# Mixture-of-experts output: rows weighted as they leave PSUM and added by an accumulating scatter to a copy of the residual in device memory

## What is computed

```
weights = g_val * e_val / sum(e_val)         # two experts of 32 for each token
y = 0
for e in range(32):
    h = silu(x2d @ w_gate[e]) * (x2d @ w_up[e])        # 1024 -> 256
    y = y + combine[:, e:e + 1] * (h @ w_down[e])      # 256 -> 1024
h = h + y                                    # the residual rows
return rmsnorm(h, final_norm_g)              # then the second block
```

## Time and profile before

| | |
|---|---|
| median of 3 runs | 1476.79 us (1476.45 to 1480.57) |
| the profiled execution | 1477.63 us, span 1475.9 us |
| PE | busy 1288.1 us, 87% of the span |
| DVE, ACT, POOL | 564.3, 479.1 and 173.1 us |
| TensorE clock granted | 0.933 of full speed in the mean |
| expert loop | from 537.95 us (first turned rows) to 790.58 us (last output stored) |

### The profile page before, as it was taken

How to read it: one execution, slowest core, us unless ns; L and a number is a source line. 1 busy time by engine, 2 the same in 40 slices (tenths; PEclk the granted TensorE clock), 3 DMA queues, 4 the chain that set the end, 5 groups by cost and what they waited for, 6 DMA issues and landing times. The chain is left out here.

```text
span 1475.9 us, 24366 instructions
## 1 busy us (share of the span) xinstructions
PE 1288.1 (87%) x10299; PEld 998.4 (68%) x10299; DVE 564.3 (38%) x1010; ACT 479.1 (32%) x806; POOL 173.1 (12%) x219
## 2 busy tenths in 40 slices
PE   5999797579986949998883699999989989899988
PEld 4888753269966735654442698888877767666668
DVE  3331132765653132322223513344438753522222
ACT  4222266612134221111112424555545533111120
POOL 4000032010004012322211001122200000000030
PEclk9999899789997969998987799999999999999989
DMA  4332000000017559999996346233152026113011
GB/s 144 114 100 72 1 0 0 14 3 4 4 59 287 201 193 367 386 390 394 390 405 228 90 152 135 77 100 96 58 73 71 30 91 226 57 57 114 0 58 58
DMA packets 92488, 195.53 MB, mean 132 GB/s; under 512 B 9510, under 2 KB 73084, under 8 KB 79452
## 3 DMA queue, kind: packets, MB, share of 16 engines
q1 hardware_dynamic: 86604, 183.48, 36.5%
q0 software_dynamic: 5200, 8.40, 1.8%
q10 hardware_dynamic: 576, 2.10, 0.4%
HBM read 184.74 MB, written 16.81 MB: 137 GB/s over the span
## 5 line engine op out<-in xcount | busy, mean ns | idle before, releaser
L1768 PE MATMUL hidden_ps<-w_gate,gathered_t 128*64 128x256 f32 x432 | 116.4, 430 | 24.1 <-DMA w_up<-exp_w_up_dram 23.3
L1768 PE MATMUL hidden_ps<-w_up,gathered_t 128*64 128x256 f32 x432 | 116.4, 430 | 0.0
L1768 PEld LDWEIGHTS hidden_ps<-w_gate,gathered_t 128*64 128x64 f32 x432 | 64.8, 156 | 62.6 <-issue 36.8
L1333 PE MATMUL wo_ps<-w_out_high,wo_x_high 128*128 128x256 f32 x256 | 75.2, 294 | 19.2 <-POOL wo_x_low L1374 19.2
L414 PE MATMUL proj_ps<-block_in_high,w_in_low 128*128 128x512 f32 x232 | 90.5, 390 | 0.0
L414 PE MATMUL proj_ps<-block_in_low,w_in_high 128*128 128x512 f32 x232 | 90.5, 390 | 0.0
L414 PE MATMUL proj_ps<-block_in_high,w_in_high 128*128 128x512 f32 x232 | 90.4, 390 | 0.0
L462 DVE TENSOR_TENSOR w_in_low<-w_in_raw,w_in_high 128x2048 fp32r<-128x2048 f32 x20 | 45.8, 2292 | 116.4 <-ACT w_in_high L454 116.4
L414 PE MATMUL gate_ps<-block_in_high,gate_w_high 128*128 128x512 f32 x192 | 79.8, 416 | 11.3 <-DVE gate_w_low L462 11.3
L414 PE MATMUL gate_ps<-block_in_low,gate_w_high 128*128 128x512 f32 x192 | 76.5, 398 | 0.0
L414 PE MATMUL gate_ps<-block_in_high,gate_w_low 128*128 128x512 f32 x192 | 76.3, 397 | 0.0
(11 more groups left out here) (456 smaller groups left out, 3147.2 us busy)
## 6 DMA issues: line engine op xcount, KB each, us to landing
w_gate<-exp_w_gate_dram SPq DMA_DIRECT2D x27, 1024.0 KB
w_up<-exp_w_up_dram SPq DMA_DIRECT2D x27, 1024.0 KB
w_down<-exp_w_down_dram SPq DMA_DIRECT2D x27, 1024.0 KB
w_in_raw<-w_in_dram SPq DMA_DIRECT2D x20, 1024.0 KB, 5.7
slot_scratch_and_keys<-w_in_dram SPq DMA_DIRECT2D x14, 1024.0 KB, 5.3
vb<-w_in_dram SPq DMA_DIRECT2D x6, 1024.0 KB, 5.6
gate_w_raw_odd<-w_in_dram SPq DMA_DIRECT2D x6, 1024.0 KB, 5.9
slot_scratch_and_keys<-exp_w_gate_dram SPq DMA_DIRECT2D x5, 1024.0 KB
```

Source lines behind the costliest of these rows:

```text
L1333: m = pe.matmul(banks[n % nb][:, 0:UNIT], x[a][k][:, c * P:(c + 1) * P], wts.parts(u, k, slice(0, UNIT))[b], start=(k == 0 and a + b == 0) ...
L1768: x = pe.matmul(g_bank[e % 2][a * CAP:(a + 1) * CAP, 0:DE], xT[e % 2][:, k, :], w[:, k, :], start=(k == 0), stop=(k == KC - 1))
```

## The change

Rows leave PSUM already multiplied with the weight of their token and expert, and the scatter adds them to rows of `token_sums_dram`, a tensor of 512 rows which starts as a copy of `h`. In its parts:

- SP writes `h` (2 MB) to `token_sums_dram` behind the last weight load of the out projection; POOL waits for it at the head of `experts`.
- The lists keep only the token's row. The second value of the marks is 1, is multiplied with the choice's weight (DVE), and a second product on PE (`weigh`, 16 matmuls, as two copies for the two halves of the partitions) gives the weight for each place: `list_weights`. It is made before the loop and again at the end of a round.
- DVE's copy becomes a multiply by a column, and ACT's copy gets a scale.
- POOL's scatter adds (`compute_op=ALU.add`). Two experts can add to the same row, so each scatter waits for the one before it.
- SP reads back 4 x 512 KB straight into `h`. The eight additions on DVE are gone; ACT squares as the chunks land.

```diff
@@ out_projection, SP; Router
                     head.store_rows(sp)
                     load_expert(sp, A, M, 5, 5)
+                    head.store_sums(sp)
+    def store_sums(self, sp):
+        sp.dma_start(self.M["sums_dram"].rearrange("(c p) d -> p c d", p=P), self.h[:, :, :]).then_inc(self.M["sums_in"], 16)
@@ Lists
     def product(self, pe, n, at, bank):
-            x = pe.matmul(bank[0:CAP, 0:2 * NE], at[:, jc, :], self.M["marks"][:, jc, :, :].rearrange("p a e -> p (a e)"),
-                          start=(jc == 0), stop=(jc == 2 * TT - 1))
+            x = pe.matmul(bank[0:CAP, 0:NE], at[:, jc, :], self.M["marks"][:, jc, 0, :], start=(jc == 0), stop=(jc == 2 * TT - 1))
+    def weigh(self, pe, n, at, bank):
+        pe.wait_ge(self.marked, n + 1)
+        for a in range(2):
+            for jc in range(2 * TT):
+                x = pe.matmul(bank[a * CAP:(a + 1) * CAP, NE:2 * NE], at[:, jc, :], self.M["marks"][:, jc, 1, :],
+                              start=(jc == 0), stop=(jc == 2 * TT - 1))
+        x.then_inc(self.weighed, 1)
+    def mark_first(self, dve, at):
+        pl = self.M["places"][:, :, :].rearrange("p j c -> p (j c)")
+        dve.tensor_scalar(pl, pl, float(CAP), None, ALU.add).then_inc(self.back, 1)
+        dve.wait_ge(self.back, 1)
+        self.mark(dve, 1, at)
+    def store_weights(self, dve, n, bank):
+        dve.wait_ge(self.weighed, n + 1)
+        dve.tensor_copy(self.weights[:, :], bank[:, NE:2 * NE]).then_inc(self.weights_in, 1)
@@ experts, SP
-                    sp.dma_start(yg[c], rows[:, c, :, :]).then_inc(got[c], 16)
+                    sp.dma_start(h[:, c, :], rows[:, c, :]).then_inc(got[c], 16)
@@ experts, POOL
+                def add_rows(e):
+                    return pool.indirect_dma_start(out=M["sums_dram"], out_offset=bass.IndirectOffsetOnAxis(ap=idx[:, e:e + 1], axis=0),
+                                                   in_=y[e % YB][:, :], in_offset=None, bounds_check=S - 1, oob_is_err=False,
+                                                   compute_op=ALU.add).then_inc(y_out[e % YB], 16)
+                pool.wait_ge(M["sums_in"], 16)
...
-                            write_rows(idx[:, e, 1:2], e)
+                            if e:
+                                pool.wait_ge(y_out[(e - 1) % YB], uses(rnd, e - 1, YB) * 16 + 16)
+                                pool.sem_inc(seen)
+                            add_rows(e)
@@ experts, PE
+                pe.wait_ge(marked, 1)
+                lists.weigh(pe, 1, at[:, :, :], h_bank[0])
                 with pe.Fori(0, rounds(pe)) as rnd:
...
-                    lists.product(pe, rnd + 1, at[:, :, :], h_bank[0])
+                    lists.weigh(pe, rnd + 2, at[:, :, :], h_bank[0])
+                    lists.product(pe, rnd + 2, at[:, :, :], h_bank[0])
@@ experts, ACT
-                    act.activation(y[e % YB][:, 512:D], y_bank[e % 2][CAP:P, :], ACT.Copy).then_inc(y_hi, 1)
+                    act.activation(y[e % YB][:, 512:D], y_bank[e % 2][CAP:P, :], ACT.Copy,
+                                   scale=lists.weights[CAP:P, e:e + 1]).then_inc(y_hi, 1)
@@ experts, DVE
-                    dve.tensor_copy(y[e % YB][:, 0:512], y_bank[e % 2][0:CAP, :]).then_inc(y_lo, 1)
+                    dve.tensor_scalar(y[e % YB][:, 0:512], y_bank[e % 2][0:CAP, :], lists.weights[0:CAP, e:e + 1], None, ALU.mult).then_inc(y_lo, 1)
...
+                    hot = M["marks"][:, :, 1, :]
+                    dve.tensor_tensor(hot, hot, w[:, :, :].rearrange("p j c -> p (j c)").unsqueeze(2).to_broadcast([P, 2 * TT, NE]),
+                                      ALU.mult).then_inc(marked, 1)
...
-                        dve.scalar_tensor_tensor(out=h[:, c, :], in0=yg[c][:, j, :], scalar=M["weights"][:, j, c:c + 1], in1=h[:, c, :],
-                                                 op0=ALU.mult, op1=ALU.add).then_inc(added, 1)
```

More of the change, by code:

```diff
@@ L1586, in __init__ @@
         self.M = M
-        self.idx = s.sb_right("list_places", [CAP, NE, 2], I32)
-        self.offs, self.placed = s.sb_right("place_offsets", [CAP, 2, NE]), s.sb_right("placed", [CAP, 2, NE])
+        self.idx = s.sb_right("list_places", [CAP, NE], I32)
+        self.offs, self.placed = s.sb_right("place_offsets", [CAP, NE]), s.sb_right("placed", [CAP, NE])
+        self.weights = s.sb_right("list_weights", [P, NE])
         self.xg = [s.sb_right(f"gathered{j}", [CAP, D]) for j in range(GB)]
@@ L1591, in __init__ @@
             s.sem("places_" + n) for n in ("marked", "less", "listed", "shifted", "stored"))
+        self.weighed, self.weights_in, self.back = s.sem("list_weights_ready"), s.sem("list_weights_stored"), s.sem("places_put_back")
         self.zeroed, self.offs_made, self.x_in = s.sem("gathered_zeroed"), s.sem("offsets_made"), s.sems("tokens_gathered", GB)
@@ L1674, in experts @@
         fin_g = M["up"][5][:, :, :].rearrange("p k n -> p (k n)")[:, 0:D]
-        rows = y_dram[0:2 * S, :].rearrange("(c p k) d -> p c k d", p=P, k=2)
-        yg = [M["gate"][j][:, :, :].rearrange("p k n -> p (k n)").rearrange("p (a d) -> p a d", a=2) for j in (4, 5, 0, 2)]
+        rows = M["sums_dram"].rearrange("(c p) d -> p c d", p=P)
         sq = [M["up"][j][:, :, :].rearrange("p k n -> p (k n)")[:, 0:D] for j in (4, 0)]
@@ L1715, in _ @@
                 for c in range(TT):
-                    sp.dma_start(yg[c], rows[:, c, :, :]).then_inc(got[c], 16)
+                    sp.dma_start(h[:, c, :], rows[:, c, :]).then_inc(got[c], 16)
             @block.gpsimd
             def _(pool):
-                def write_rows(places, e):
-                    return pool.indirect_dma_start(out=y_dram, out_offset=bass.IndirectOffsetOnAxis(ap=places, axis=0),
-                                                   in_=y[e % YB][:, :], in_offset=None, bounds_check=2 * S - 1,
-                                                   oob_is_err=False).then_inc(y_out[e % YB], 16)
+                def add_rows(e):
[3 more added lines that the diff above has]
+                pool.wait_ge(M["sums_in"], 16)
                 pool.sem_inc(places_free)
@@ L1878, in choice_weights @@
                     dve.wait_ge(weighed, 6)
+                    hot = M["marks"][:, :, 1, :]
+                    dve.tensor_tensor(hot, hot, w[:, :, :].rearrange("p j c -> p (j c)").unsqueeze(2).to_broadcast([P, 2 * TT, NE]),
+                                      ALU.mult).then_inc(marked, 1)
                 choice_weights()
+                lists.mark_first(dve, at[:, :, :])
+                lists.store_weights(dve, 0, h_bank[0])
+                dve.wait_ge(lists.weights_in, 1)
                 dve.wait_ge(M["gain_in"], 16)
@@ L1896, in _ @@
                     dve.wait_ge(places_free, rnd + 2)
-                    lists.mark(dve, rnd + 1, at[:, :, :])
+                    lists.mark(dve, rnd + 2, at[:, :, :])
                     lists.store(dve, rnd + 1, h_bank[0])
+                    lists.store_weights(dve, rnd + 1, h_bank[0])
                 dve.wait_ge(gain_in, 16)
@@ L1904, in gain @@
                     dve.tensor_tensor(h[:, c, :], h[:, c, :], fin_g, ALU.mult).then_inc(gained, 1)
-                for c in range(TT):
-                    dve.wait_ge(got[c], 16)
-                    for j in range(2):
-                        if j:
-                            dve.wait_ge(added, 2 * c + 1)
-                        dve.scalar_tensor_tensor(out=h[:, c, :], in0=yg[c][:, j, :], scalar=M["weights"][:, j, c:c + 1], in1=h[:, c, :],
-                                                 op0=ALU.mult, op1=ALU.add).then_inc(added, 1)
-                    if c:
-                        gain(c - 1)
+                for c in range(1, TT):
+                    gain(c - 1)
                 dve.wait_ge(squared, TT)
```

24 lines of the change are left out of this document (12 added, 12 removed).

## The result

| | before | changed |
|---|---|---|
| median of 4 runs each | 1477.0 us (1476.45 to 1480.57) | 1499.49 us (1493.25 to 1501.55) |
| ratio | 1 | 1.0147, 95% interval 1.0123 to 1.0172 |
| the profiled execution | 1477.63 us, span 1475.9 | 1500.56 us, span 1499.1 |
| TensorE clock granted, mean | 0.933 | 0.929 |

The change costs 22.5 us, 1.5%, and the interval is clear of 1. The forecast had the direction and a range that holds the time (1474 to 1515), but a sum of +10.6, less than half of what came.

What follows compares the result with a forecast made beforehand. The prediction took the DMA engines to bound the expert loop and the instruction chain both ends; +2.5 + 10.8 + 0 + 1.5 - 4.2 = +10.6 on 1477.63 gave 1488.2, and a median 0.8 lower, 1487.5 us, range 1474 to 1515.

Steps and rivals of the forecast that it cites:

- a sum of +10.6: Whole kernel: +2.5 head, +10.8 fetch, 0 chain, +1.5 last scatters, -4.2 tail, in us on the profiled 1477.63.
- The head: Ahead of the expert loop: `weigh` and the copy delay first gate and up by +2.5 us, bounds +0.9 and +4.2.
- The fetch: Expert loop: fetching each row's old value for the add costs DMA time like a plain move, +10.8 us.
- 15 to 20%: Expert loop: predicted q0 share, up from 9.8%, as a sign of the forecast.
- Rival (a): Expert loop: the fetch of the old row hides, sum -0.2, time 1476.6 us; chance 0.23.
- The chain: Expert loop: each scatter waits for the one before, 7 us under load; cost 0 up to 7.4 us an add.
- rival (c): Expert loop: the chain of scatters becomes the bound, 1511 us at 8.5 us an add, 1542 at 9.5; chance 0.22.
- the lower figures (3.6): Expert loop: argued landing time of 3.6 us, a gather on idle DMA engines, once a bounding chain leaves gaps.
- the forecast at 0.45: Expert loop: DMA-paced, with a cost of 5 to 16 us, time 1482 to 1494; chance 0.45.
- its second sign: Expert loop: a DMA share under 1, if the chain of scatters is the bound.
- The tail: Read-back to factors: eight additions leave, but the wait for `weigh` takes most back; 815.9 against 820.09, -4.2 us.
- The last stretch: End of the loop: the last two chained scatters leave and land later, +1.5 us counted of 2.3.

Runs made afterwards that it cites:

- experiment 4: The kernel before, with only the 2 MB store of `h` added behind the out projection's last weight load: 1482.07 us, ratio 1.0032.
- experiment 6: The changed kernel, with the copy of `h` issued behind the barrier and awaited only before the first scatter: 1489.29 us, ratio 1.0098.
- Experiment 2: The kernel before, with its scatter made adding but unchained, into 1024 separate rows: 1489.97 us, ratio 1.0091.
- experiment 12: The changed kernel, with all three refills of expert weights cut evenly to 128 KB instead of 1 MB: 1439.99 us, ratio 0.9751.
- 13: The changed kernel, with all three refills of expert weights cut to a half, 512 KB each: 1439.21 us, ratio 0.9742.
- experiment 3: The kernel before, with the scatter both adding and chained, each waiting for the one before: 1499.38 us, ratio 1.0150.
- experiment 5: The changed kernel, with experts reordered across groups and each scatter waiting only for the fourth before it: 1486.23 us, ratio 1.0063.
- experiment 11: The changed kernel with reordered experts, looser chain, later copy, later `weigh`, SP's second-block load behind the read-back, and plain writes replacing adds: 1469.46 us, ratio 0.9934.
- 8: The changed kernel with reordered experts, looser chain, later copy, later `weigh`, and SP's second-block load behind the read-back: 1483.76 us, ratio 1.0041.
- experiment 9: The changed kernel, with only the down matrix's refill cut to 128 KB on 16 partitions: 1495.82 us, ratio 1.0113.

## Why the prediction was half right

**The head: right in its own terms, with one omission.** `weigh` took 3.19 us for 3.9 forecast, gate and up started 8.70 us behind the barrier instead of 6.25 (+2.45, forecast +2.5). The size is in part luck: +2.5 lay between bounds, the lower of which had the clock up early. It stayed at 0.50 up to 548 us and beyond, `weigh` was 0.7 cheaper, and the copy landed at 542.3 and not at 540. What I left out is that the barrier itself would come late. I followed the copy only to the semaphore on which POOL waits, and gave it no effect on the gather that shares the DMA engines with it. The barrier came 3.2 us late with that gather (experiment 4; undone in experiment 6).

**The fetch: right.** The forecast of +10.8 stood on the upper bound, a fetch that costs what a move costs. Experiment 2 showed +10.3 from first to last scatter (+12.4 in the kernel's time); q0's share rose to 13.7% there and 12.3% in the changed kernel, where I had named 15 to 20%. Rival (a), with a fetch that hides, is refuted.

**The chain: this step failed.** I wrote "I take 7 under load" and "Cost 0 up to 7.4 us an add". Three things were wrong with it. The 7 us counted the transfer but little of what lies between a landing and the next issue: plain writes landed in 6.8 us and made steps of 7.7. The add put another 0.8 on the step. And against rival (c) I argued that "as soon as the chain is the bound the DMA engines have gaps, and then the lower figures (3.6) hold". They did not: the share stayed at 1.01. In the changed kernel the lower figure, a step of 4.3 us, came only when no weight was left to load. The experiments 12 and 13 show the argument's premise true, gaps do shorten the add, and its conclusion false, since the full-sized weights leave no gap: an expert's load takes 9.1 us, a step 8.7 (experiment 3). The chain decides all the same because it has 31 steps and the loop only 26 loads; that is also why it does so from a step as short as 7.4. In the kernel before, the 78.34 MB of the earlier trace rows are 8.8 us an expert, and 26 x 8.8 = 229 us are the 31 x 7.4 of its writes.

So it was rival (c) that came, at 0.22, in place of the forecast at 0.45. Its sign (POOL's wait for a DMA ahead of each scatter, steps over 7.4) was named rightly, and its second sign, a share under 1, wrongly. Its sum comes out 3 us high: with the measured mean step of 8.27 it is 1477.6 + 2.5 + 31 x (8.27 - 7.41) - 4.2 + 1.5 = 1504 for a profiled 1500.6. That is luck in part, since the barrier (+3.2) is missing from it and both ends of the tail were shorter than it says. The 26.5 us of the loop hold the fetch and the chain together, and neither alone gives them: undoing the chain gave back 12.4 of the 22.5 us (experiment 5), undoing the fetch then 15.8 (experiment 11, from 8), both by the ratios.

**The tail: right in kind, undersized.** Read-back to factors was 7.1 us shorter, forecast 4.2. (In that forecast the last short steps are 0.3 us too long: 819.05 to 820.09 are 1.0 and not 1.3.) ACT started 3.25 us behind the read-back (forecast 3.5). The lists and `weigh` were through sooner, so the first gain was done at 7.1 us (forecast 8.7), and ACT's six squares behind it took 7.0 us, not 8.1. The last stretch, scatter to read-back, was 3.8 us for a forecast of more than 6.4, because the chain had by then pushed the last scatter past SP's load; that load's delay is in the step from 810.87.

**The rule that the prediction weighed.** The Trainium skill (DMA: Bandwidth & Descriptors, Anatomy of one DMA) would give a scatter of 128 KB an estimated 2.3 us. No run agrees, and the measurement decides: the shortest add landed in 3.4 us and the median under full weights in 7.8. The chain follows a rule of the Trainium skill (DMA: Bandwidth & Descriptors, Rules for kernel authors), to wait for the earlier DMA's semaphore before an accumulating DMA touches the same bytes. No run here shows what would be lost without it; the wait cost 9.4 us (experiment 3 less 2) on top of the add.

**What stays open.** Why experiment 6 gained more than the 4.7 us of the stage; whether it is the first gather that holds the barrier, as ten traces suggest; what gives back part of the chain's cost outside the stage; and what made the adds of experiment 9 as long as those beside full weights.

## What to carry to other kernels

A chain of transfers in a loop is priced by its step under the load of that loop, with the time from landing to the next issue in it, and not by a wait or by a transfer on idle queues. Count the steps of each stream too: where the first tiles are loaded ahead, the chain has more steps than the loop has loads, can be the bound while the DMA share reads full, and shows only in the waits and in the backlog behind the last load. An accumulating scatter cost the DMA engines about its rows once more: where DMA bytes are the bound, saving vector work outside it does not pay for that, and where it must be chained, ordering the work so that neighbours touch different rows gives back most of the chain. And bytes that nobody waits for still delay a small transfer on the same engines that somebody does wait for.

## What the runs showed of the hardware

- An adding scatter took 1.41 us of POOL as an instruction, a plain one 0.92.
- The packets of POOL's queue took 4.1 to 4.3 us of 16 engines for a MB of gathers and adds together, 3.0 with plain writes.
- The same add landed in 3.8, 5.5 or 7.8 us (medians) at a DMA share of 0.41, 0.87 or 1.01, but in 8.8 at 0.92 in experiment 9.
- A 2 MB store near the end of a block delayed the engines' start in the next block by 3.3 us, though it landed only 2.6 us after that start. POOL's last gather landed in 6.9 us beside it, in 3.6 without, and in ten kernels the start came 0.4 to 0.5 us behind that landing.
- A load of 128 KB landed in 13.9 us behind two loads of 1 MB in SP's queue (experiment 9, over 16 partitions), in 2.4 behind two of 128 KB (experiment 12, over 128). Which of the two, queue or partitions, makes the difference no run tells.
